# TensorE's order in the attention steps: the values of the step before ahead of the scores of three steps on

## The reference

```
scores = einsum('bnqkgd,bnskd->bnkgqs', qb, kb) * HEAD_DIM ** -0.5     # a block of 128 queries, 256 keys
scores = where(valid, scores, NEG_INF)
probs  = softmax(concatenate([scores, sink], -1), -1)[..., :-1]
out    = einsum('bnkgqs,bnskd->bnqkgd', probs, vb)
```

## Time and profile before

| | |
|---|---|
| median of 3 runs | 1988.67 us (1988.25 to 1991.69) |
| the profiled execution's own time | 1989.11 us |
| its span, first to last instruction | 1987.3 us |
| granted TensorE clock, mean | 0.999 |
| PE busy | 1928.8 us (97%) |
| DVE busy | 1432.1 us (72%) |
| ACT busy | 910.1 us (46%) |
| POOL busy | 464.8 us (23%) |
| scores (L1583), first and last start | 998.0 and 1109.4 us |
| transposes of the probabilities (L1637), first and last start | 1015.8 and 1120.9 us |

### The profile page before, as it was taken

How to read it: one execution, slowest core, us unless ns; L and a number is a source line. 1 busy time by engine, 2 the same in 40 slices (tenths; PEclk the granted TensorE clock), 3 DMA queues, 4 the chain that set the end, 5 groups by cost and what they waited for, 6 DMA issues and landing times.

```text
span 1987.3 us, 28820 instructions
## 1 busy us (share of the span) xinstructions
PE 1928.8 (97%) x9238; PEld 1584.2 (80%) x9238; DVE 1432.1 (72%) x2388; ACT 910.1 (46%) x1738; POOL 464.8 (23%) x464
## 2 busy tenths in 40 slices
PE   6899999999999999999999999999999999999998
PEld 6778888888888878888866687788888888888787
DVE  5987777777777786576578748777777777777863
ACT  4654443444444454343268645444444344443531
POOL 2312222222122221010036312122222221212310
PEclk9999999999999999999999999999999999999999
DMA  5232323233332250231000113233232323335201
GB/s 198 100 113 91 90 84 95 79 100 95 95 95 90 90 201 25 67 111 54 0 12 1 59 48 106 85 90 106 90 91 83 95 79 100 95 96 182 98 28 68
DMA packets 214761, 173.29 MB, mean 87 GB/s; under 512 B 8608, under 2 KB 196384, under 8 KB 214688
## 3 DMA queue, kind: packets, MB, share of 16 engines
q1 hardware_dynamic: 212960, 166.08, 26.3%
q10 hardware_dynamic: 1728, 6.29, 1.0%
HBM read 159.75 MB, written 12.58 MB: 87 GB/s over the span
## 4 chain that ended last, share of the span: by engine, by line
PE 85%; DVE 8%; POOL 2%; issue 2%; DMA 1%; ACT 1%; SPq 0%; DVEq 0%; ACTq 0%; POOLq 0%
PE ps L783 13%; PE ps L784 13%; PE ps L785 13%; PE ps L295 7%; PE ps L297 7%; PE ps L296 7%; PE ps L882 6%; PE ps L881 6%; PE ps L880 6%; POOL probs L1629 1%; PE ps L356 1%; DVE ps L1594 1%; PE ps L1583 1%; PE ps L1637 1%; PE ps L593 1%
## 5 line engine op out<-in xcount | busy, mean ns | idle before, releaser
L1205 DVE TENSOR_TENSOR H<-H,ps 128x512 f32<-128x512 f32 x496 | 328.1, 686 | 112.8 <-PE ps L882 111.9
L1067 POOL TENSOR_TENSOR s_raw<-s_raw,a_raw 128x512 f32<-128x512 f32 x66 | 87.5, 1327 | 766.5 <-DVE s_lo L1118 649.5
L783 PE MATMUL ps<-t_hi,s_hi 128*128 128x512 f32 x528 | 206.6, 391 | 7.2 <-DVE t_lo L1217 4.2
L784 PE MATMUL ps<-t_lo,s_hi 128*128 128x512 f32 x528 | 205.7, 390 | 0.0
L785 PE MATMUL ps<-t_hi,s_lo 128*128 128x512 f32 x528 | 205.7, 390 | 0.0
L956 ACT ACTIVATE m<-ps 128x512 f32<-128x512 f32 x44 | 26.4, 599 | 266.0 <-PE ps L785 263.6
L784 PE MATMUL ps<-b_lo,a_hi 128*128 128x512 f32 x352 | 137.1, 390 | 0.0
L785 PE MATMUL ps<-b_hi,a_lo 128*128 128x512 f32 x352 | 137.1, 390 | 0.0
L783 PE MATMUL ps<-b_hi,a_hi 128*128 128x512 f32 x352 | 137.1, 389 | 0.0
L882 PE MATMUL ps<-wd_hi,d_ab_lo 128*128 128x512 f32 x336 | 130.9, 389 | 0.0
L880 PE MATMUL ps<-wd_hi,d_ab_hi 128*128 128x512 f32 x336 | 130.8, 389 | 0.0
(11 more groups left out here) (290 smaller groups left out, 5148.7 us busy)
## 6 DMA issues: line engine op xcount, KB each, us to landing
a_raw<-in_w_ff_gate SPq DMA_DIRECT2D x88, 256.0 KB, 3.0
a_raw<-in_w_ff_up SPq DMA_DIRECT2D x88, 256.0 KB, 3.0
s_raw<-in_w_ff_up SPq DMA_DIRECT2D x88, 256.0 KB, 2.9
s_raw<-in_w_ff_gate SPq DMA_DIRECT2D x88, 256.0 KB, 3.0
wd_raw<-in_w_ff_down SPq DMA_DIRECT2D x44, 512.0 KB, 4.3
residual_spill<-H SPq DMA_DIRECT2D x16, 512.0 KB, 2.8
raw<-in_w_ple_gate SPq DMA_DIRECT2D x16, 512.0 KB, 4.5
back<-residual_spill SPq DMA_DIRECT2D x16, 512.0 KB, 4.7
```

Of the source, the lines that this page charges most:

```text
L783: pe.matmul(ps[:, bank, :], w[0], x[0], start=fresh and k == 0, stop=False, skip_group_check=not fresh)
L784: pe.matmul(ps[:, bank, :], w[0], x[1], start=False, stop=False, skip_group_check=not fresh)
L1067: eng.tensor_tensor(form_raw(name), W_RAW[name][:, :, :], form_raw(other) if other != "A21" else W_RAW["A21"][:, :, :], op).then_inc(summe ...
L1205: dve.tensor_tensor(dst, dst, src, ALU.add).then_inc(F["summed"], 1)
```

## The change

In each iteration of TensorE's loop the call of `values` for n-1 moves from behind `scores` for n+3 to ahead of it. Nothing is added or removed, and no other engine's program changes: the orders of VectorE, ScalarE, GpSimd and SyncE are the same.

```
                 turn_probs(pe, n)
+                if n >= 1:
+                    values(pe, n - 1)
                 if n + 3 < STEPS_A:
                     scores(pe, n + 3)
-                if n >= 1:
-                    values(pe, n - 1)
             values(pe, STEPS_A - 1)
```

## The result

The changed kernel takes 2002.21 us (median of 4 runs, 2001.65 to 2004.05), the kernel before 1988.46 (4 runs beside it): the medians are 13.8 us apart. The ratio is 1.0064, 95% interval 1.0052 to 1.0076, which is 12.7 us (10.3 to 15.1). The forecast was 2002.0, +13.3.

A forecast was written before the change was run, and what follows sets the result against it. Taken as bound: a ring through POOL, TensorE and DVE, 6.49 us per two steps. 14 turns x 1.02 = +14.3, less 1.0 for a shorter stall, gives +13.3: 2002.0 us against the median, range 1998.5 to 2004.5.

The forecast's parts named there:

- The ring through POOL, TensorE and DVE over two steps: Attention steps: transposes, scores, row maximum, sink gap, reciprocal, normalisation close a turn of 6.49 us over two steps, values left out.
- TensorE at 98% busy: Rival: TensorE's occupancy, 38.17 of 39.00 us, bounds the steps, so order costs nothing: 1988.7 us; no difference had chance 0.05.
- The size of s: Block of values put into the ring between transposes and scores: 1.02 us taken, range 0.80 to 1.07.
- New waits: Values of n-1, now ahead of scores, wait for both copies of n-1 and `att_out` of n-3: cost 0.
- The uneven pattern: Normalisations: step 2 stays, step 3 moves by s, so even to odd takes 4.26 us, the other 3.24.
- DVE's wait: Sign in the steps: DVE's wait for the scores (L1583) 28 times about 1.4 us instead of 0.38.
- The stall beside `o_first_lo`: DVE's small instruction (L1599) beside that POOL operation loses 0.31 us instead of 1.33, giving 1.02 us back.
- What follows: Behind step 29: old order, output projection keeps TensorE busy 60.00 of 60 us, so no wait absorbs the delay.
- The slack of ScalarE: Exponentials of step 11 end 0.45 us before DVE takes their sum; that slack stays in the new order.
- The clock: Granted clock in the steps stays at 1.00, as where PE is 89% busy; priced at nothing.
- the rival: Clock falls to 1.2 GHz in the steps: 14 turns x 3.1 = 43 us more, 2045 us; chance 0.02.
- The range: Whole kernel: 1998.5 to 2004.5 us, from s of 0.80 to 1.07, an unshortened stall, and 0.5 at each end.

The follow-up runs named there:

- half_before: Kernel before with its order kept, each block of values cut to the products with its own keys (4 records instead of 8): ratio 0.9998 against the kernel before.
- half_after: Changed order with the same halved blocks of values (4 records instead of 8): ratio 1.0042 against the kernel before, total +8.2 us.
- odd_only: Kernel before with values moved ahead of scores in the odd iterations only, 14 of the 28: ratio 1.0060, total +11.8 us.
- pairs: Kernel before with values moved ahead of scores where n % 4 is 1 or 2, 14 of the 28 iterations: ratio 1.0027, total +5.4 us.
- split_before: Kernel before with its order kept, normalisation in two halves, the first four transposes waiting for the first half only: ratio 0.9990, total -2.1 us.
- recip3_before: Kernel before with TensorE's order kept, on VectorE the sum and reciprocal moved ahead of the fourth maximum: 2024.07 us in one run, total +35.3.

## Why the prediction was right

- *What bounds the steps.* Right. The ring through POOL, TensorE and DVE over two steps, and not TensorE at 98% busy: half_before took work from TensorE and gained nothing, half_after paid for the block by its length, odd_only and pairs show the two rings, split_before that TensorE's bound lies at 3.10.
- *The size of s.* 1.02 was taken, and 1.01 to 1.02 is measured, in 14 turns of each ring.
- *New waits.* None came; the values start 1.02 behind the transposes, as the scores did.
- *The uneven pattern.* 3.24 and 4.26 forecast, 3.24 and 4.25 measured (1026.45 to 1029.69, 1022.20 to 1026.45); the normalisation of 2 stays 3.25 behind that of 1. Behind step 19 the pattern is 3.10 and 4.40, two steps still 7.50.
- *DVE's wait.* Wrong in the list of signs: 28 waits of about 1.4 us were forecast, and from 1023 to 1062 us only every second one is 1.40, the others 0.39 or 0.40; from 1010 to 1125 they are 24.1 us in 27 waits instead of 39. The uneven pattern asks for that: a turn is 1.02 longer over two steps, and one of its two waits takes it all. It changes nothing in the sum.
- *The stall beside `o_first_lo`.* 0.31 us forecast, from 0.16 to 0.50 measured, 0.34:

```profile
1085.89 0.50 DVE L1599 TENSOR_TENSOR small<-sinks_placed,small 128x4 f32<-128x4 f32 x1
...
1086.42 0.21 ACT L1608 ACTIVATE sink_exp<-small 128x4 f32<-128x4 f32 x1 [0.60 <-DVE small L1599]
```

- *What follows.* Right: 874.9 us behind step 30 in both. That they agree to 0.1 is luck in part, for the other kernels with whole blocks of values need from 874.1 to 876.4 there.
- *The slack of ScalarE.* It did not stay at 0.45 but grew: in the changed kernel the exponentials of step 9 end at 1047.03 and DVE takes their sum at 1048.49, those of step 10 at 1050.63 and 1051.72. So they never hold the reciprocal in these steps.
- *The clock.* Priced at nothing, and in the steps of the changed kernel it was 1.00. But the ground given was thin: "PE at 89% with the clock at 1.00" was a stretch that ended at 1225, and the row of 1223 to 1227 above, of the same kernel, has 0.75, behind the 2.2 us without a matmul that rows 9 hold. half_after shows a fall in the steps themselves, one stretch for 1.2 us, where the rival had 43 us for all 14 turns. The better ground came only with recip3_before, 72% busy with the clock at 1.00. What makes the clock fall in one execution and not in another is not shown.
- *The total.* +13.3 forecast; the steps have +13.2, the medians +13.8, the ratio +12.7. The mechanism and its terms earn the +13.2. That a total comes so near is luck in part, since the start of an execution alone moves it by 1.8 us. The range was added up a little too wide at its top: 1988.7 + 15.0 + 0.5 is 2004.2 and not 2004.5.

## What to carry to other kernels

An engine that is 98% busy in a stretch need not be its bound, as here. Look for a ring through the others: add up the times from one instruction's start to the next one's along the waits until you are back at an instruction of the first kind, and see over how many steps the ring closes. In this kernel, work behind the instruction for which another engine waits was free because it fitted into the wait that follows; the same work ahead of it was paid once for each turn of the ring. To decide where the bound is, shorten the suspected work by half and look whether the period moves.

## What was not expected of the hardware

The granted clock fell in some executions and not in others, and at different places. From 38 to 60 us it was 0.88 to 0.90 in five of the ten profiled executions, with either order, and step 1 then starts at 1018.4 to 1019.1 us; in the other five it was 1.00 and step 1 starts at 1015.8 to 1017.2. In half_after it was 0.56 in one stretch of the steps, for 1.2 us. That is as much as the smaller effects of this case, and it is why differences between profiles were taken from step 1 to step 30 and not from the spans.

Cutting an operation of POOL in two cost only 0.15 us in all (2.04 against 1.89).
